# Two column strips for the sample's probability-times-value products

## The reference, cut to what matters

```
o_cmp = einsum('bkgtn,bnkd->btkgd', p_cmp, vc)
o = block(...)  # selected: einsum('bkgqm,bkqmd->bqkgd', p, vg)
o = block(...)  # window:   einsum('bkgqm,bmkd->bqkgd', p, v_win)
o = gates[:, :, 0] * o_cmp + gates[:, :, 1] * o_sel + gates[:, :, 2] * o_win
```

## Time and profile before

| what | us |
|---|---|
| median of three runs | 3053.54 |
| the profiled execution, its own time | 3052.95 |
| span of its trace | 3051.2 |
| PE busy, of the span | 2739.9 (90%) |
| DVE, ACT busy | 1292.4 (42%), 698.9 (23%) |
| selected-page products (L1414), both layers | 129.0 |

### The profile page before, as it was taken

One profiled execution on the slowest core, in us unless ns is written; L12 is line 12 of the kernel. 1 busy time (PEld: TensorE's weight loads), 2 busy tenths in 40 slices (PEclk: granted clock), 3 DMA queues, 4 the chain that ended last, 5 costly groups with the idle time before them and its releaser, 6 DMA issues. The chain is left out here.

```text
span 3051.2 us, 40719 instructions
## 1 busy us (share of the span) xinstructions
PE 2739.9 (90%) x14224; PEld 2174.7 (71%) x14224; DVE 1292.4 (42%) x2967; ACT 698.9 (23%) x1675; POOL 318.7 (10%) x320
## 2 busy tenths in 40 slices
PE   7988999699598899999989889996977987999997
PEld 6866777467495678888768667775757856888886
DVE  2723555454444654301047255554544357442012
ACT  0122444222421121100011244442242112111001
POOL 0500000000030311001124000000001203110010
PEclk9987999899795899999989889997987758999998
DMA  6214555143003032333032165542420110323220
GB/s 194 70 53 153 177 186 181 41 135 112 2 6 93 14 89 80 90 106 78 0 108 69 43 218 172 172 127 74 135 67 1 51 48 14 111 83 97 56 56 30
DMA packets 335231, 273.99 MB, mean 90 GB/s; under 512 B 52977, under 2 KB 330802, under 8 KB 334698
## 3 DMA queue, kind: packets, MB, share of 16 engines
q1 hardware_dynamic: 308632, 252.63, 27.8%
q10 hardware_dynamic: 26450, 19.37, 2.2%
HBM read 262.08 MB, written 18.17 MB: 92 GB/s over the span
## 5 line engine op out<-in xcount | busy, mean ns | idle before, releaser
L2360 PE MATMUL psum<-ff,HT 128*128 128x272 f32 x1536 | 353.3, 392 | 0.0
L437 PE MATMUL psum<-xT,ring 128*128 128x272 f32 x1408 | 328.8, 397 | 25.3 <-PEq L163 25.3
L2360 PEld LDWEIGHTS psum<-ff,HT 128*128 128x128 f32 x1536 | 291.8, 190 | 60.2
L437 PEld LDWEIGHTS psum<-xT,ring 128*128 128x128 f32 x1408 | 270.7, 193 | 82.3 <-issue 25.8
L1035 PE MATMUL psum<-chunks,W 128*128 128x512 f32 x512 | 242.2, 635 | 10.6 <-DVE chunks L1157 10.6
L1157 DVE COPY chunks<-psum 64x256 f32<-64x256 f32 x512 | 215.3, 421 | 30.3 <-PE psum L1014 23.0
L2214 PE MATMUL psum<-yT,HT 128*128 128x272 f32 x896 | 215.7, 398 | 0.0
L1014 PE MATMUL psum<-cst,ring 128*128 128x128 f32 x1536 | 193.3, 278 | 19.7 <-DMA ring<-in_cache_nsa_kv 19.6
L1035 PEld LDWEIGHTS psum<-chunks,W 128*128 128x128 f32 x512 | 102.5, 203 | 138.6 <-issue 138.6
L2214 PEld LDWEIGHTS psum<-yT,HT 128*128 128x128 f32 x896 | 172.7, 193 | 36.3
L1014 PEld LDWEIGHTS psum<-cst,ring 128*128 128x128 f32 x1536 | 177.8, 147 | 28.9 <-DMA ring<-in_cache_nsa_kv 21.5
(11 more groups left out here) (485 smaller groups left out, 3964.8 us busy)
## 6 DMA issues: line engine op xcount, KB each, us to landing
ring<-in_cache_nsa_kv SPq DMA_DIRECT2D x512, 192.0 KB, 3.5
ring<-in_w_up SPq DMA_DIRECT2D x32, 1024.0 KB, 5.5
ring<-in_cache_nsa_kv SPq DMA_DIRECT2D x384, 64.0 KB, 2.0
HT<-in_w_down SPq DMA_DIRECT2D x12, 2048.0 KB, 9.1
ring<-in_w_in SPq DMA_DIRECT2D x20, 1024.0 KB, 5.2
ring<-in_cache_nsa_kv ACTq DMA_DIRECT2D x128, 64.0 KB, 2.3
HT<-in_w_out SPq DMA_DIRECT2D x8, 1024.0 KB, 5.1
yT<-in_w_down SPq DMA_DIRECT2D x4, 2048.0 KB, 12.5
```

Of the source, the lines that this page charges most:

```text
L437: last = pe.matmul(psum[0:w.shape[1], 2 * (t % 3) + h, 0:HALF], w, S.xT[:, k, h * HALF:(h + 1) * HALF], start=(k == 0), stop=(k == KT - 1))
L2360: last = pe.matmul(out[h], down[t % 3][:, k, :], f[:, k, x], start=(k == 0), stop=(k == FT - 1))
```

## The change

The products of a sequence go alternately to two strips of 32 partitions of the same PSUM bank (0 to 31 and 32 to 63): even pages to the first, odd ones to the second, and likewise for the block's products. A strip is 32 columns wide, so 32 columns of probabilities are loaded, those of the sequence and of its neighbour in a pair. The block's order becomes window, compressed, new tokens, with the window's wait ahead of it. The copy to `o_s` takes 64 partitions, and instead of a transpose a product with a table of ones and zeros, `pick`, takes the sequence's 16 rows from each strip and adds them.

```diff
+    t["pick"] = i[:2 * 32, None] % 32 == np.arange(32)[None, :]
...
-    o_s = sb("o_s", [16, NB, P], ctx=ctx)
+    o_s = sb("o_s", [64, NB, P], ctx=ctx)
...
-                cols = slice(16 * b, 16 * b + 16)
-                o = psum[0:16, 6 + b % 2, 0:P]
+                cols = slice(32 * (b // 2), 32 * (b // 2) + 32)
+
+                def strip_of(c):
+                    return psum[32 * c:32 * c + 32, 6 + b % 2, 0:P]
+
                 if h == 0 and third == 0:
                     if b >= 2:
                         pe.wait_ge(s.s_copied, b - 1)
-                    pe.matmul(o, S.pt_new[:, 0, cols], S.kv_s[:, 3 * P:4 * P], start=True, stop=False)
-                    pe.matmul(o, S.pt_new[:, 1, cols], S.kv_s[:, 5 * P:6 * P], start=False, stop=False)
+                    pe.wait_ge(s.window, 16 * b + 16)
+                    for j in range(4):
+                        pe.matmul(strip_of(j % 2), S.st_win[:, j, cols], vwin[:, j, :], start=(j < 2), stop=False)
                     for j in range(2):
                         m = P - j
-                        pe.matmul(o, S.pt_cmp[0:m, j, cols], S.vc[0:m, j, b, :], start=False, stop=False)
-                    pe.wait_ge(s.window, 16 * b + 16)
-                    for j in range(4):
-                        pe.matmul(o, S.st_win[:, j, cols], vwin[:, j, :], start=False, stop=False)
+                        pe.matmul(strip_of(j), S.pt_cmp[0:m, j, cols], S.vc[0:m, j, b, :], start=False, stop=False)
+                    pe.matmul(strip_of(0), S.pt_new[:, 0, cols], S.kv_s[:, 3 * P:4 * P], start=False, stop=False)
+                    pe.matmul(strip_of(1), S.pt_new[:, 1, cols], S.kv_s[:, 5 * P:6 * P], start=False, stop=False)
...
-                    last = pe.matmul(o, S.st_sel[:, half * h + t, cols], vsel[:, h, t, :], start=False, stop=(h == 1 and t == half - 1))
+                    last = pe.matmul(strip_of(t % 2), S.st_sel[:, half * h + t, cols], vsel[:, h, t, :], start=False,
+                                     stop=(h == 1 and t >= half - 2))
...
-                last = pe.transpose(psum[:, 7, 16 * b:16 * b + 16], o_s[:, b, :], C["ident"][0:16, 0:16])
+                last = pe.matmul(psum[:, 7, 16 * b:16 * b + 16], o_s[:, b, :], C["pick"][:, 16 * (b % 2):16 * (b % 2) + 16],
+                                 start=True, stop=True)
...
-                act.copy(o_s[:, b, :], psum[0:16, 6 + b % 2, 0:P]).then_inc(s.s_copied, 1)
+                act.copy(o_s[:, b, :], psum[0:64, 6 + b % 2, 0:P]).then_inc(s.s_copied, 1)
```

## The result

The changed kernel takes 3085.01 us (median; 3082.58 to 3088.7), the kernel before 3055.14 us in the same runs: a ratio of 1.0096, with an interval of 1.0078 to 1.0113. It is about 30 us slower; 3029 us was forecast.

The account below looks back on a forecast made before the run. SP's issuing was taken to bound early sequences, PE late ones. Savings of 7.1 us in distances, 1.3 at the start and 3.5 at the end made 11.9 a layer, 24 in all: 3029 us, own range 3024 to 3040, 8-in-10 range 3021 to 3056.

Parts of the forecast that it names:

- What bounds the kernel: In the attention-output stage, early sequences are bound by SP's issuing of page transfers, late ones by PE.
- SP's floor of 17.0 us: Shortest distance between window transfers that SP's issuing allows, put between 16.6 and 17.0 us, taken as 17.0.
- Two strips: Alternating page products overlap in part: five save 0.30 us, six 0.375, the closing run of 22 saves 1.58.
- The step of 0.143 us a product: Time from one overlapped product to the next: 0.109 us streaming plus 0.034 us load, instead of 0.218 us.
- Rival 1: Loads ahead of time, strips overlap fully: 0.109 us a product, 30 us saved in all, 3023 us; chance 0.20.
- Block order and pick product: Block ahead of each sequence: net 0.36 us saved after one more row change of about 0.09; pick product costs nothing.
- The step that failed: Clock remark after the stage's sum: more 1.2 GHz stretches, hidden where SP limits, taking back some us where PE does.
- The sign that was named for it: Among the signs of a right forecast: more idle time of PE put down to the page transfers; no size given.
- no overlap (2): Strips share the moving operand's feed, products stay 0.109 us an instruction, row changes add 1.4 us: 3054 us; chance 0.25.
- draining (3): Every change of strip empties the array at 0.09 us, 544 changes, 49 us on PE: 3102 us; chance 0.08.
- a floor of 17.8 us for SP (4): SP takes nearly everything: 9.6 us a layer saved, 3034 us; chance 0.46 together with the main forecast.
- The slower case: A result slower than the kernel before, chance 0.08, all of it from every strip change emptying the array.

Follow-up runs that it names:

- a3: Changed kernel with strips alternating from product to product only in sequences 5, 6 and 7: 3047.59 us, ratio 0.998.
- b4: Changed kernel with the old block order and no overlap in sequences 0 to 4, overlap in 5 to 7: 3037.21 us, ratio 0.9959.
- c2: Changed kernel with the old block order and no overlap in sequences 0 to 3, overlap from sequence 4 on: 3035.54 us, ratio 0.994.
- a1: Changed kernel without overlap: block and first half of the pages to strip 0, second half to strip 1; 3067.9 us, ratio 1.0041.
- b3: Changed kernel without overlap in any sequence and with the block order of the kernel before: 3059.66 us, ratio 1.0023.
- a2: Changed kernel without overlap in sequence 0, strips alternating in sequences 1 to 7: 3113.15 us, ratio 1.0192.
- b1: Kernel before (one strip, 16 columns) without the products of every second page, transfers and waits kept: 3036.63 us, ratio 0.9943.
- c1: Changed kernel, sequence 0 in old order without overlap; in sequences 1 to 7 SP fetches only 4 of 12 pages a half: 3000.43 us, ratio 0.9827.
- c3: Changed kernel, overlap everywhere, with SP fetching only the first 4 of 12 pages a half in sequences 1 to 7: 3023.27 us, ratio 0.9884.
- b2: Changed kernel with strips alternating only in sequences 0 to 2: 3068.65 us, ratio 1.0059.
- a4: Changed kernel with one more f32 product of 128 by 128 ahead of each unit's transposes, 48 a layer: 3079.43 us, ratio 1.0069.

## Why the prediction was wrong

- **What bounds the kernel**: right. PE bounds the late sequences and SP the early ones; the late distances of a3, b4 and c2 come down to 16.7 to 17.7 us (one of c2 stays at 19.7), about SP's floor of 17.0 us.
- **Two strips**: the mechanism was right, the size too small. The step of 0.143 us a product assumed that the two instructions of one product follow each other before the other strip starts; in fact the first instructions of two products start together. Rival 1, full overlap, was the nearer: it had savings of 0.44 us for five and 0.545 for six, the groups show 0.42 and 0.63 (0.30 and 0.375 were forecast).
- **Block order and pick product**: wrong in size. The order was put at 0.09 us for one change of row height; with the clock's first rise it costs a1 some 6 us a layer against b3 in the profiled executions (172.6 and 171.3 us for 166.6 and 165.0). By the ratios it is nearer 3 us a layer, and their intervals overlap; the rise itself comes after 24 to 27 us in both layers of a1, a2 and a3, and after 17 us in those of the kernel before, b1, b3, b4, c1 and c2. The pick product was put at nothing and costs 1.3 us a layer.
- **The step that failed** is the last one of the sum: "A PE that waits for SP more often could have more of them; where SP is the limit that is hidden, where PE is it may take back some us." The direction was seen, and the sum had no term for it. The two stages were to become 24 us shorter and the kernel became 30 us slower, so the missing term is some 54 us (an estimate, from the medians). Three things in the sentence failed. It tied the low clock to more waiting for pages; PE waited 1.9 and 2.8 us for them instead of 2.3 and 2.4, and still stretches at 1.2 GHz grew from 20 to 120 us in layer 0 and from 17 to 147 in layer 1. It took the price to be some us; the first stretch grew from 17 to 58 us without a wait for pages, and the second lasted 61 and 89 us behind one wait of 1.3 and 2.5 us, right into the sequences where PE is the limit, at 7 to 9 us a sequence. And it took the time to be hidden where SP is the limit; there it was 2 to 3 us a sequence, so that by the window transfers sequence 3 began 4 to 6 us later in the stage than before. The sign that was named for it, more idle time of PE put down to the pages, did not come.
- **The rivals**: no overlap (2) and draining (3) are refuted by the first rows after; a floor of 17.8 us for SP (4) is refuted by the late distances of b4 and c2. The slower case that came was none of them. Its chance, 0.08, belonged to a mechanism that did not happen, so the slower result was missed altogether.

What is shown: the overlap brings the long low stretches (a1, without it, has the clock back at 0.90 and 0.92), and without page waits and SP's limit the overlap runs at the full clock from the first rise on (c1, c3). What is argued and not shown: that a wait by itself *causes* a fall. In the profiles every fall between the first rise and the last 4 us of a stage comes within a wait of PE or up to 2.2 us behind one, but not every wait has one: a1 waits 2.43 us for pages in layer 1 and b2 1.78 us, without a fall. What differs is what comes after. With one strip, page waits of 1.6 to 2.4 us left the clock low for 3.4 to 6.9 us or not at all (before, a1, a3, b2, b3, b4, c2). In overlapped sequences, waits of 0.9 to 2.6 us left it low for 17 to 89 us in the changed kernel, a2 and a4, for 3.4 and 6.8 us in late sequences of a3 and c2, and some not at all. What in the overlapped stretches keeps the clock low after a wait has ended is open. With 48 products more a layer the first stretch is 41 us instead of 58 (a4), without the overlap in the later sequences there is no second one (b2), and one strip with half of the page products has such stretches too (b1).

## What to carry to other kernels

A shorter product on PE is worth its saving only while the granted clock stays up. Where the clock is low at a stage's start, and where PE meets waits, set a price for the time after them too, at the lower clock, and not only for the wait's length; and read the granted clock by stretches after the change. Here the overlap paid where PE is the limit and hardly waits (sequences 5 to 7: b4, 0.4% faster) and not where a queue is the limit. The order of the block at a stage's start was worth some 3 to 6 us a layer, though nothing in its instructions said so: it moved the first rise of the clock by 7 to 10 us.

## What was not expected of the hardware

Products of f32 in two column strips of 32 run side by side almost without loss: a run of 12 instructions lasts 0.85 us instead of 1.48, and the first instructions of two products that stand one behind the other in the program start within 0.01 us. A product with an f32 table that gives 128 by 16 takes two instructions where the transpose to the same shape takes one (16 in 1.93 us for 8 in 0.64). And the clock can stay at 1.2 GHz for 88.7 us while PE is busy for 87.65 us of them; ten overlapped instructions then last 1.49 us, longer than 1.26 us one behind the other at 2.4 GHz.
